# Residual rows read early into the experts' weight buffers, and a final stage that adds in place there

## The reference

```
x3 = x2 + cross_attention(...)
y  = top-2 of 64 experts for each token, each (silu(h@Wg) * (h@Wu)) @ Wd
out = rmsnorm(x3 + w0*y0 + w1*y1, g_final)
```

## Time and profile before

| what | value |
|---|---|
| median of 3 runs | 3102.77 us (3102.7 to 3104.42) |
| the profiled execution, its own time | 3101.34 us |
| its span | 3099.5 us |
| PE busy | 2713.6 us, 88% |
| DVE busy | 1605.9 us, 52% |
| ACT busy | 1278.0 us, 41% |
| first instruction of the final stage | 3001.00 us |

### The profile page before, as it was taken

The page is one execution under the profiler, slowest core; times in us unless marked ns, Lnnn a source line. Parts: engine busy times, 40 slices in busy tenths (PEclk is TensorE's granted clock), DMA queues, the critical chain, the costliest instruction groups (busy, mean ns, idle before and its releaser), DMA issues. The chain is left out here.

```text
span 3099.5 us, 37499 instructions
## 1 busy us (share of the span) xinstructions
PE 2713.6 (88%) x12694; PEld 2072.7 (67%) x12695; DVE 1605.9 (52%) x2113; ACT 1278.0 (41%) x2101; POOL 615.9 (20%) x710
## 2 busy tenths in 40 slices
PE   7999999999969999994999975899837999999960
PEld 5787777787746666673999963677635777776640
DVE  3624425325256665653444413554466777776637
ACT  4334333333236666763111103442205555565534
POOL 0000000000035555644222200000003222234410
PEclk9999999999969999996999987899868999999985
DMA  4353443533421121105344323222245999999958
GB/s 158 101 177 120 137 153 102 168 122 113 146 50 37 42 57 36 36 11 170 119 140 139 122 92 113 82 104 82 93 190 220 360 361 362 362 372 357 352 212 352
DMA packets 166828, 505.47 MB, mean 163 GB/s; under 512 B 40480, under 2 KB 69408, under 8 KB 138560
## 3 DMA queue, kind: packets, MB, share of 16 engines
q1 hardware_dynamic: 148288, 470.49, 43.9%
q0 software_dynamic: 18432, 33.60, 3.0%
HBM read 430.14 MB, written 107.28 MB: 173 GB/s over the span
## 5 line engine op out<-in xcount | busy, mean ns | idle before, releaser
L577 DVE TENSOR_TENSOR fr_wl<-fr_raw,fr_wh 128x1024 fp32r<-128x1024 f32 x128 | 156.8, 1225 | 465.6 <-ACT fr_wh L462 465.2
L2307 DVE TENSOR_TENSOR ex_gl<-ba_raw,ex_gh 128x2048 fp32r<-128x2048 f32 x128 | 289.9, 2290 | 140.6 <-ACT ex_gh L2238 138.9
L462 ACT CAST fr_wh<-fr_raw 128x1024 fp32r<-128x1024 f32 x128 | 134.0, 1047 | 497.2 <-PE fr_acc L388 493.0
L388 PE MATMUL fr_acc<-fr_hh,fr_wh 128*128 128x512 f32 x1024 | 272.1, 408 | 2.0 <-DVE fr_hl L593 2.0
L2238 ACT CAST ex_gh<-ba_raw 128x2048 fp32r<-128x2048 f32 x128 | 240.1, 1907 | 80.1 <-PEq L1867 41.8
L958 ACT ACTIVATE at_pf<-at_psS 128x512 f32<-128x512 f32 (+1 forms) x320 | 178.3, 558 | 185.1 <-PE at_psS L865 100.4
L388 PE MATMUL fr_acc<-fr_hh,fr_wl 128*128 128x512 f32 x1024 | 254.4, 391 | 0.0
L388 PE MATMUL fr_acc<-fr_hl,fr_wh 128*128 128x512 f32 x1024 | 253.3, 389 | 0.0
L1057 POOL TENSOR_TENSOR at_pl<-at_pf,at_ph 128x512 fp32r<-128x512 f32 (+1 forms) x160 | 193.5, 1210 | 257.4 <-ACT at_ph L959 256.9
L2202 PE MATMUL ex_psY<-ba_raw,ex_hT 128*128 128x512 f32 x512 | 231.9, 595 | 5.8 <-issue 4.6
L388 PEld LDWEIGHTS fr_acc<-fr_hh,fr_wh 128*128 128x128 f32 x1024 | 193.9, 191 | 56.0 <-issue 15.3
(11 more groups left out here) (323 smaller groups left out, 5231.7 us busy)
## 6 DMA issues: line engine op xcount, KB each, us to landing
ba_raw<-in_w_exp SPq DMA_DIRECT2D x192, 1024.0 KB, 16.7
fr_raw<-in_w_slabs SPq DMA_DIRECT2D x128, 512.0 KB, 4.1
gates_d<-fr_gst SPq DMA_DIRECT2D x64, 256.0 KB, 4.6
mx_gt<-gates_d SPq DMA_DIRECT2D x64, 256.0 KB, 5.3
cb_ys<-y_d SPq DMA_DIRECT2D x16, 1024.0 KB, 9.3
xa_xe<-x_d SPq DMA_DIRECT2D x18, 512.0 KB, 5.2
mx_xr<-in_x SPq DMA_DIRECT2D x8, 1024.0 KB, 7.1
x_d<-mx_xo SPq DMA_DIRECT2D x8, 1024.0 KB, 5.1
```

The costliest lines, as they stand in the source:

```text
L388: mm = nc.tensor.matmul(acc[i % 2][:], w[:, i % 2, k, :], h[:, q % 2, k, :], start=(j == 0 and k == 0), stop=(j == 2 and k == KD - 1))
L2307: V.tensor_tensor(gl[:, s, i], raw[:, r, i, :].rearrange("p (k n) -> p k n", k=KD // 2), gh[:, s, i], ALU.subtract).then_inc(w_lo, 1)
```

## The change

The residual rows no longer have buffers of their own. At the end of the expert stage SP reads all of x3 into the slots 1 to 3 of `raw`, which belonged to the experts 61 to 63: eight transfers of 1 MB, each of two tiles, each after the wait that says that this part of the slot has been read. The final stage gets `raw` and the eight semaphores `x3_in`, and adds in place in `raw`. It has six buffers of `ys` and three of `yo`, and its loops are written out. The first transfer is now `ys` of tile 0, the second is `gb`; DVE waits for `gb` only before its first scaling. The loads of tile i+6 wait for tile i to be added, and stand before the store of tile i on SP. The square's output, which nobody reads, is bf16; ACT has one more wait, on a reciprocal two tiles back.

```diff
+            for j in range(NT // 2):
+                r, i = 1 + j // 3, j % 3
+                e = E - RAW + r
+                if i < 2:
+                    sp.wait_ge(w_lo, 2 * e + i + 1)
+                else:
+                    sp.wait_ge(down, e + 1)
+                sp.dma_start(raw[:, r, i, :].rearrange("p (t d) -> p t d", d=D),
+                             x3_d[2 * j * P:2 * (j + 1) * P, :].rearrange("(t p) d -> p t d", p=P)).then_inc(x3_in[j], 16)
...
-    R = 4
+    R = 6
-        xr = s_.sb("xr", [P, R, D])
-        sq = s_.sb("sq", [P, D])
-        yo = s_.sb("yo", [P, 2, D])
+        sq = s_.sb("sq", [P, D], BF16)
+        yo = s_.sb("yo", [P, 3, D])
...
+        def x_tile(i):
+            return raw[:, 1 + i // 6, i % 6 // 2, i % 2 * D:(i % 2 + 1) * D]
...
+            def load(i):
+                if i >= R:
+                    sp.wait_ge(added, i - R + 1)
+                sp.dma_start(ys[:, i % R].rearrange("p a d -> p (a d)"), y_rows[i]).then_inc(y_in[i % R], 16)
+            def store(i):
                 sp.wait_ge(done, i + 1)
+                sp.dma_start(out[i * P:(i + 1) * P, :], yo[:, i % 3, :]).then_inc(stored[i % 3], 16)
+            load(0)
             sp.dma_start(gb[:], g.broadcast_to([P, D])).then_inc(g_in, 16)
+            for i in range(1, R):
+                load(i)
+            for i in range(NT):
+                if i + R < NT:
+                    load(i + R)
+                store(i)
...
-            dve.wait_ge(g_in, 16)
+            def add(i):
+                if i % 2 == 0:
+                    dve.wait_ge(x3_in[i // 2], 16)
+                dve.wait_ge(y_in[i % R], 16 * (i // R + 1))
+                V.scalar_tensor_tensor(x_tile(i), ys[:, i % R, 0, :], wts[:, i, 0:1], x_tile(i), ALU.mult, ALU.add).then_inc(first_added, 1)
                 dve.wait_ge(first_added, i + 1)
+                V.scalar_tensor_tensor(x_tile(i), ys[:, i % R, 1, :], wts[:, i, 1:2], x_tile(i), ALU.mult, ALU.add).then_inc(added, 1)
+            def norm(i):
                 dve.wait_ge(rms_done, i + 1)
+                V.reciprocal(st[:, i % 2, 2:3], st[:, i % 2, 1:2]).then_inc(rcp_done, 1)
                 dve.wait_ge(rcp_done, i + 1)
+                if i >= 3:
+                    dve.wait_ge(stored[i % 3], 16 * (i // 3))
+                if i == 0:
+                    dve.wait_ge(g_in, 16)
+                V.scalar_tensor_tensor(yo[:, i % 3, :], x_tile(i), st[:, i % 2, 2:3], gb[:], ALU.mult, ALU.mult).then_inc(done, 1)
...
+            for i in range(NT):
+                act.wait_ge(added, i + 1)
+                if i >= 2:
+                    act.wait_ge(rcp_done, i - 1)
+                nc.scalar.activation(sq[:], x_tile(i), ACT.Square, accum_out=st[:, i % 2, 0:1]).then_inc(sq_done, 1)
```

More of the change, by code:

```diff
@@ L2041, in _, with experts @@
             link(V.tensor_copy(meta[:, 0:32], psK[0:1, 0:32]))
-def experts(nc, cst, h_d, w_exp, y_d, tab, rows, meta, raw, r_in):
+def experts(nc, cst, h_d, x3_d, w_exp, y_d, tab, rows, meta, raw, r_in, x3_in):
     with ExitStack() as ctx:
@@ L2352, in _, with combine @@
             overflow(dve, more)
-def combine(nc, x3_d, y_d, wts, g, out):
-    R = 4
+def combine(nc, raw, x3_in, y_d, wts, g, out):
+    R = 6
     with ExitStack() as ctx:
         s_ = Scope(nc, ctx, "cb")
-        xr = s_.sb("xr", [P, R, D])
         ys = s_.sb("ys", [P, R, 2, D])
-        sq = s_.sb("sq", [P, D])
-        yo = s_.sb("yo", [P, 2, D])
+        sq = s_.sb("sq", [P, D], BF16)
+        yo = s_.sb("yo", [P, 3, D])
         gb = s_.sb("gb", [P, D])
@@ L2366, in combine @@
         eps = s_.sb("eps", [P, 1])
-        x_in = [s_.sem(f"x_in{i}") for i in range(R)]
         y_in = [s_.sem(f"y_in{i}") for i in range(R)]
-        stored = [s_.sem(f"stored{i}") for i in range(2)]
+        stored = [s_.sem(f"stored{i}") for i in range(3)]
         g_in, eps_set, first_added, added, sq_done, rms_done, rcp_done, done = (s_.sem(n) for n in (
@@ L2373, in combine @@
         block = ctx.enter_context(nc.Block())
+        def x_tile(i):
+            return raw[:, 1 + i // 6, i % 6 // 2, i % 2 * D:(i % 2 + 1) * D]
         @block.sync
         def _(sp):
[L2377 to L2381, removed]
-                sp.wait_ge(done, i + 1)
[L2383 to L2388, removed]
-            sp.dma_start(gb[:], g.broadcast_to([P, D])).then_inc(g_in, 16)
[L2390 to L2410, removed]
+            def load(i):
[3 more added lines that the diff above has]
+            def store(i):
+                sp.wait_ge(done, i + 1)
+                sp.dma_start(out[i * P:(i + 1) * P, :], yo[:, i % 3, :]).then_inc(stored[i % 3], 16)
+            load(0)
+            sp.dma_start(gb[:], g.broadcast_to([P, D])).then_inc(g_in, 16)
+            for i in range(1, R):
[4 more added lines that the diff above has]
+                store(i)
+            for e in range(3):
+                sp.wait_ge(stored[e], 16 * ((NT - e + 2) // 3))
         @block.vector
@@ L2415, in _ @@
             V.memset(eps[:], EPS).then_inc(eps_set, 1)
-            dve.wait_ge(g_in, 16)
[L2418 to L2422, removed]
+            def add(i):
[3 more added lines that the diff above has]
+                V.scalar_tensor_tensor(x_tile(i), ys[:, i % R, 0, :], wts[:, i, 0:1], x_tile(i), ALU.mult, ALU.add).then_inc(first_added, 1)
                 dve.wait_ge(first_added, i + 1)
-                V.scalar_tensor_tensor(xr[:, r, :], ys[:, r, 1, :], wts[:, bass.ds(i, 1), 1], xr[:, r, :], ALU.mult, ALU.add).then_inc(added, 1)
-            def norm(t, s):
-                i = R * t + s
+                V.scalar_tensor_tensor(x_tile(i), ys[:, i % R, 1, :], wts[:, i, 1:2], x_tile(i), ALU.mult, ALU.add).then_inc(added, 1)
+            def norm(i):
                 dve.wait_ge(rms_done, i + 1)
-                V.reciprocal(st[:, s % 2, 2:3], st[:, s % 2, 1:2]).then_inc(rcp_done, 1)
+                V.reciprocal(st[:, i % 2, 2:3], st[:, i % 2, 1:2]).then_inc(rcp_done, 1)
                 dve.wait_ge(rcp_done, i + 1)
-                dve.wait_ge(stored[s % 2], 16 * (R // 2) * t + 16 * (s // 2 + 1))
-                V.scalar_tensor_tensor(yo[:, s % 2, :], xr[:, s % R, :], st[:, s % 2, 2:3], gb[:], ALU.mult, ALU.mult).then_inc(done, 1)
-            tiles(dve, add, norm)
+                if i >= 3:
[3 more added lines that the diff above has]
+                V.scalar_tensor_tensor(yo[:, i % 3, :], x_tile(i), st[:, i % 2, 2:3], gb[:], ALU.mult, ALU.mult).then_inc(done, 1)
+            add(0)
+            for i in range(NT):
+                if i + 1 < NT:
+                    add(i + 1)
+                norm(i)
         @block.scalar
@@ L2439, in _ @@
             act.wait_ge(eps_set, 1)
[L2440 to L2447, removed]
+            for i in range(NT):
+                act.wait_ge(added, i + 1)
+                if i >= 2:
+                    act.wait_ge(rcp_done, i - 1)
+                nc.scalar.activation(sq[:], x_tile(i), ACT.Square, accum_out=st[:, i % 2, 0:1]).then_inc(sq_done, 1)
+                act.wait_ge(sq_done, i + 1)
+                nc.scalar.activation(st[:, i % 2, 1:2], st[:, i % 2, 0:1], ACT.Sqrt, bias=eps[:], scale=1.0 / D).then_inc(rms_done, 1)
 def program(nc, a, out):
@@ L2507, in program @@
             route(nc, cst, lg, wts, tab, rows, meta, load_first_experts)
-            experts(nc, cst, h_d, a["w_exp"], y_d, tab, rows, meta, raw, r_in)
-            combine(nc, x3_d, y_d, wts, a["g_final"], out)
+            x3_in = [b_.sem(f"x3_in{i}") for i in range(NT // 2)]
+            experts(nc, cst, h_d, x3_d, a["w_exp"], y_d, tab, rows, meta, raw, r_in, x3_in)
+            combine(nc, raw, x3_in, y_d, wts, a["g_final"], out)
 def constants():
```

## The result

The changed kernel takes 3085.75 us in the median of 4 runs (3081.3 to 3089.18), the kernel before 3102.73 (4 runs, 3100.49 to 3104.42). The ratio is 0.9945, with a 95% interval of 0.9928 to 0.9962. That is 17.0 us faster, by the interval 12 to 22, where 25.4 had been forecast. The time lies above the forecast range of 3074 to 3084. Two later sets of five runs, on two chips, give 3082.45 against 3103.78 and 3085.33 against 3104.78, thus 21.3 and 19.5 us, both with a ratio of 0.9935 (0.9921 to 0.9948 and 0.9922 to 0.9949).

A forecast was written before the change was run, and what follows sets the result against it. Transfers were taken to bind the final stage, after a late start waiting for `gb`. 3009.7 + 54.9 + 8.7 + 0.8 = 3074.1 against a span of 3099.5, so 3102.8 − 25.4 = 3077.4 us; range 3074 to 3084.

The forecast's parts named there:

- The bound before, and the early start: Final stage: transfers bind at 4.86 us a tile; without awaiting `gb`, the second tile's first add comes 13.0 us earlier.
- The two terms of my sum: Final stage: 13.0 us from the earlier start and 13.2 us from 14 tiles at 3.92 instead of 4.86 us.
- DVE becomes the bound at 3.92 us a tile: Final stage: transfers need only 3.74 us a tile, under DVE's 3.92, so 14 tiles take 13.2 us less.
- The transfers still bind: Rival, final stage: at 363 GB/s a tile takes 4.33 us, the run about 3083.5 us; chance 0.1.
- Three output buffers just suffice: Final stage: store 0 lands 0.1 to 0.9 us before the fourth scaling needs its buffer; cost 0, bound 0.5 us.
- The end of the stage, written-out loops, table loads: Final stage: 8.7 us from last first add to end, unchanged; loops and table loads priced at nothing, square unchanged at 1.06.
- Code arrives late: Rival, final stage: straight-line code fetched while DMA engines are full costs up to 9.4 us, giving 3086.8; chance 0.07.
- The scatter, the step that failed: End of expert stage: the last scatter of `y`, sharing with residual transfers, costs 0.8 us.
- The sign named for it: Wrong if the time from the last scatter's issue to SP's first final-stage load, 4.6 us before, grows beyond 6.
- the upper bound: Last scatter: at most 4.7 us, what a gather pays beside the weights, 8.7 against 4.0 us landing.
- The gain as a whole: Whole kernel: 25.4 us less, from 3102.8 to 3077.4 us.
- The gain at the start is partly lost: Rival: the last three residual loads hold the scatter and first `ys`; 4.7 instead of 0.8 us, thus 3081.3; chance 0.1.

The follow-up runs named there:

- e4: Kernel before with only `gb` loaded behind the first tile's `ys` and awaited by the scalings, not the first add: 3093.69 us, ratio 0.9966.
- e7: Changed kernel with two output buffers instead of three: 3089.05 us in one run.
- e3: Changed kernel with the last three residual transfers moved from the expert stage into SP's queue of the final stage: 3082.47 us, ratio 0.9936.
- e1: Changed kernel run once more without an edit: 3082.45 us, ratio 0.9935 to the kernel before.
- e12: Changed kernel with three more 1 MB transfers behind the eight residual ones, into slot 0 of `raw`, where nobody reads them: 3086.60 us in one run.
- e2: Changed kernel with residual transfers reordered, all halves first and the two third parts last: 3079.84 us, ratio 0.9928.
- e8: Changed kernel with six residual halves asked for early, two third parts in the final stage, six output buffers: 3079.66 us, ratio 0.9916.

## Why the prediction was wrong, step by step

**The bound before, and the early start.** Right as a whole. The second tile's first add was to come 8.7 us after SP's first load and came at 9.6. The 13.0 us can't be had alone, though: e4 gives 8.7, the length of the hole. The two terms of my sum hold only together, since the stage stays bound by transfers without the move.

**DVE becomes the bound at 3.92 us a tile.** Right: 3.91, at 424 GB/s. "The transfers still bind" falls for this kernel. By the lower figure of the Trainium skill (DMA: Bandwidth & Descriptors, Bandwidth: about 358 GB/s) DVE would have waited for `ys` or for buffers all along; it waited for neither after the second tile.

**Three output buffers just suffice.** Right: store 0 landed 9.6 us after its issue at 3027.95 (forecast 9.5 to 10.3), thus at 3037.6, 23.2 us after SP's first load (forecast 22.3 to 23.1). DVE never waited for it, and e7 and e3 show both ways of losing the margin.

**The end of the stage, written-out loops, table loads.** Right: 8.72 us at the end. There is one table load in the stage, where two were forecast and eight had been. The square with bf16 output takes 1057 ns, as before. "Code arrives late" falls, as DVE has no idle time in the stage beyond its two waits for `ys`. The final stage as a whole was forecast at 72.3 us and took 73.0.

**The scatter, the step that failed.** The text says: "here the neighbours end near 2999.8 at the latest", and takes 0.8 us, the scatter's bytes at the full rate. It measured 4.1 (8.70 against 4.63), 4.5 in e1. The sign named for it came: the time from the last scatter's issue to SP's first load grew beyond 6. With e3 the cause is shown: without the neighbours it is 4.48. The row that had the price was at hand: a gather beside the weights lands in 8.7 us and alone in 4.0, a difference of 4.7, which I kept only as the upper bound.

Three things were wrong in setting it aside. First, the neighbours didn't end in time. The sum has SP's three transfers alone, ending 3.4 us after the last scatter's issue; they ended 6.8 us after it. It leaves out the scatter before the last one, issued 4.35 us earlier and moving beside the same transfers, and takes the full 421 GB/s where the windows have 384 and 387. Second, e12 shows that the price of a busy neighbour does not follow from how many bytes are shared: it is there in full with 3 MB and no larger with 6. The Trainium skill's rule of turns between queue rows (DMA: Bandwidth & Descriptors, Queues, rings and completion order) agrees with e12 in that more volume does not hold the scatter longer; it gives no price, and the conclusion that it supports 0.8 was mine and false. Third, the room was smaller than the share said. The 0.15 at 2970 to 2980 was the tail of the weights up to 2976, with a scatter beside it, and all engines idle only from 2977 on. e2 shows what such a tail does: its last scatter takes 3.6 us to move what takes 1.3 alone. Why a scatter's data begins 2.3 to 2.6 us later beside SP's transfers stays open.

**The gain as a whole.** With 4.1 for 0.8 and 73.0 for 72.3 the sum is −25.4 + 3.3 + 0.8 = −21.3 us. That would have been 3081.5, inside the range. The three measured differences are 17.0, 21.3 and 19.5. So of the miss of 8.4 us in the first set 4.1 are steps of the forecast, and 4.3 are the spread between executions, here bad luck: they lie within the set's interval, and stages that the change doesn't touch moved by up to 7 us between profiles. It was the forecast's second error to give 1.5 us for that: the runs of the changed kernel alone range over 8.

**The rivals.** "The gain at the start is partly lost" is the case that came: 3081.3 forecast, at a chance of 0.1. Half of its mechanism is the one measured: the residual loads held the scatter, but not the first `ys`, which landed as forecast, on engines that had been empty for 2 us. No other occurred.

**Open.** Which DMA engines are behind at the end of the expert loop, and why, was not tried; the packets tell how many move at a time, not which. e4 shows that a loop can be 3.1 us longer than in the one profile of before with the same expert code; whether a us of it belongs to the change in the others can't be told.

## What to carry to other kernels

When transfers are moved into an idle stretch, look for what else must land there, and price a transfer on another queue by a row in which it has such neighbours, not by its bytes. List every transfer that moves in that stretch, not only the last. A low DMA share is not room for a whole transfer: 0.18 was three engines fully busy here; look at the landing of the last one issued. An earlier start in a stage bound by transfers gains no more than the hole in its queue, so test it alone before relying on it.

## What the runs showed of the hardware that was not expected

A scatter of 0.33 MB issued by POOL has moved its data 2.9 us after its issue on idle engines, and 6.9 to 7.4 us after it beside SP's transfers, whether these are 3 or 6 MB; it begins later (3.8 to 4.1 us instead of 1.6) and moves more slowly (3.1 to 3.6 us instead of 1.3). After 192 weight transfers the DMA works on for some 8 us with about three packets in flight where a full window has 16 (87 and 78 GB/s at shares of 0.22 and 0.18 from 2968 to 2973, the last weights landing at 2976.2), and such a tail stands again behind 6 MB more (e8: 77 GB/s at 0.19). The final stage keeps 424 to 425 GB/s for 40 us with loads and stores two to one.
